# Hybrid decoder trunk, one core: queries and keys of two of four retention heads by Strassen's block form

## The reference

```
xn = rmsnorm(x) * ln_gain
q, k, v, z_a, x_b, z_b, g_a, g_b = split(xn @ w_in)
q, k = rope(q), rope(k) * 256**-0.5             # 4 heads; q, k 256 wide, v 512 wide
A = group_norm(retention(q, k, v, state)) * silu(z_a)   # 128-token chunks, a decaying 256 x 512 state a head
B = rglru(causal_conv4(x_b)) * silu(z_b)                # width 1536
x = x + (sigmoid(g_a) * (A @ w_a) + sigmoid(g_b) * (B @ w_b)) @ w_o
```

## Time and profile before

| | |
|---|---|
| median of 3 runs | 1893.31 us (1891.85 to 1895.51) |
| profiled execution, span from first to last instruction | 1889.0 us (its own time outside the span is not shown) |
| TensorE busy | 1872.9 us, 99% |
| VectorE busy | 1306.7 us, 69% |
| ScalarE busy | 827.0 us, 44% |
| GpSimd busy | 298.6 us, 16% |
| moved by DMA | 264.06 MB, mean 140 GB/s |

### The profile page before, as it was taken

How to read it: one execution, slowest core, us unless ns; L and a number is a source line. 1 busy time by engine, 2 the same in 40 slices (tenths; PEclk the granted TensorE clock), 3 DMA queues, 4 the chain that set the end, 5 groups by cost and what they waited for, 6 DMA issues and landing times.

```text
span 1889.0 us, 32627 instructions
## 1 busy us (share of the span) xinstructions
PE 1872.9 (99%) x13004; PEld 1755.0 (93%) x13004; DVE 1306.7 (69%) x2260; ACT 827.0 (44%) x1352; POOL 298.6 (16%) x417
## 2 busy tenths in 40 slices
PE   9999999999999999999999999999999999999998
PEld 8899898898899999999998988988988999999997
DVE  7775665665766877866797656657557678878575
ACT  5432322423436776543444324234124377766334
POOL 2220120120231210100132201202102422001010
PEclk9999999999999999999999999999999999999999
DMA  6444534553443333543655445534444534337253
GB/s 220 137 129 159 179 132 130 163 180 110 150 147 96 104 99 99 155 134 105 199 175 162 148 124 170 178 110 152 168 119 146 167 97 107 96 93 183 90 167 116
DMA packets 119958, 264.06 MB, mean 140 GB/s; under 512 B 12510, under 2 KB 52942, under 8 KB 119678
## 3 DMA queue, kind: packets, MB, share of 16 engines
q1 hardware_dynamic: 87950, 159.94, 27.3%
q0 software_dynamic: 31712, 102.04, 17.5%
q10 hardware_dynamic: 144, 0.00, 0.0%
HBM read 203.11 MB, written 49.12 MB: 134 GB/s over the span
## 4 chain that ended last, share of the span: by engine, by line
PE 87%; DVE 5%; ACT 3%; DMA 2%; DVEq 1%; issue 1%; ACTq 1%; SPq 0%
PE bank L2414 19%; PE bank L2416 19%; PE bank L2415 19%; PE bank L2508 4%; PE bank L2509 4%; PE bank L2510 4%; PE bank L2778 2%; PE bank L2781 2%; PE bank L2780 2%; DMA w_raw<-in_w_units 2%; PE sums L2526 2%; PE sums L2508 1%; PE sums L2510 1%; PE sums L2509 1%; PE sums L2641 1%
## 5 line engine op out<-in xcount | busy, mean ns | idle before, releaser
L2414 PE MATMUL bank<-xn_hi,w_hi 128*128 128x296 f32 (+1 forms) x2016 | 603.5, 299 | 1.1 <-DVEq L2324 0.5
L2416 PE MATMUL bank<-xn_lo,w_hi 128*128 128x296 f32 (+1 forms) x2016 | 598.9, 297 | 0.0
L2415 PE MATMUL bank<-xn_hi,w_lo 128*128 128x296 f32 (+1 forms) x2016 | 598.1, 297 | 0.0
L2414 PEld LDWEIGHTS bank<-xn_hi,w_hi 128*128 128x128 f32 x2016 | 379.0, 188 | 8.4 <-issue 6.0
L671 ACT ACTIVATE w_hi<-w_raw 128x1024 fp32r<-128x1024 f32 x219 | 230.2, 1055 | 349.0 <-DMA w_raw<-in_w_units 346.4
L2415 PEld LDWEIGHTS bank<-xn_hi,w_lo 128*128 128x128 f32 x2016 | 379.5, 188 | 0.9
L2416 PEld LDWEIGHTS bank<-xn_lo,w_hi 128*128 128x128 f32 x2016 | 378.6, 188 | 0.0
L681 DVE TENSOR_TENSOR w_lo<-w_raw,w_hi 128x1024 fp32r<-128x1024 f32 x219 | 268.4, 1229 | 59.1 <-ACT w_hi L671 52.5
L2414 PE MATMUL bank<-oa_hi,w_hi 128*128 128x296 f32 (+1 forms) x512 | 153.7, 300 | 0.0
L2415 PE MATMUL bank<-oa_hi,w_lo 128*128 128x296 f32 (+1 forms) x512 | 151.9, 297 | 0.0
L2416 PE MATMUL bank<-oa_lo,w_hi 128*128 128x296 f32 (+1 forms) x512 | 151.7, 296 | 0.0
(11 more groups left out here) (347 smaller groups left out, 3846.1 us busy)
## 6 DMA issues: line engine op xcount, KB each, us to landing
w_raw<-in_w_units SPq DMA_DIRECT2D x189, 512.0 KB, 3.7
w_raw<-in_w_units SPq DMA_DIRECT2D x151, 256.0 KB, 3.4
S<-in_state_ret POOLq DMA_DIRECT2D x64, 512.0 KB, 4.8
out_ret_s<-S POOLq DMA_DIRECT2D x64, 512.0 KB, 6.2
w_raw<-in_w_units POOLq DMA_DIRECT2D x20, 256.0 KB, 4.9
vst<-v_scr SPq DMA_DIRECT2D x8, 512.0 KB, 4.1
out_ret_p<-Sp POOLq DMA_DIRECT2D x8, 512.0 KB, 5.9
v_scr<-vtok_hi SPq DMA_DIRECT2D x16, 160.0 KB
```

Source lines behind the costliest of these rows:

```text
L2414: pe.matmul(ps, w_hi[:, slot, cols], x_hi, start=first, stop=False)
L2415: pe.matmul(ps, w_lo[:, slot, cols], x_hi, start=False, stop=False)
L2416: return pe.matmul(ps, w_hi[:, slot, cols], x_lo, start=False, stop=last)
```

## The change

For the third and the fourth head of each layer (`PAIR_HEADS = (2, 3)`), queries and keys are made by the block form: first the pair of key tiles, then the pair of query tiles, 7 x 12 matmuls each in place of 2 x 48. On all 592 tokens in both layers.

- **Token sums.** The four sums are made once a layer on VectorE: two steps at the end of the first head, six among the second head's queries and keys (`token_sum`), in six planes over `vo` and the value places. POOL stores four of them to DRAM in the second head (`store_sums`), and both ScalarE and VectorE wait for these stores before the values' tail is written.
- **Reload.** At the end of the second and third head, after the last transposes, POOL loads the four planes (592 KB each) back into the same places (`load_sums`). ScalarE makes four high parts; VectorE makes the low parts of DIFF and MIX2 after the second unit of W_A and those of EDGE and LAST after the fourth.
- **Weights.** SP loads 14 raw parts in place of four units. POOL adds into S1 of the keys' pair behind `load_sums`, into S3 of the keys' behind the last state stores, into S1 of the queries' ahead of the next head's state loads, and into S3 of the queries' behind them.
- **End of a head before a changed one.** ScalarE and VectorE split A11, S1, S2, A12 of the keys in place of three units, VectorE also makes S2 + S1 and S4 + S2.
- **In the head.** `high_pairs` and `low_pairs` are written out for ScalarE and VectorE. The keys are turned (`turned`) among the queries' parts, the queries after the last product. `keys(0)` waits for the keys alone; the wait for the queries moves to before `cross(0)`.
- `act.sem_inc` and `dve.sem_inc` for units held by pairs become a drain that increments.
- `product`, `part_high`, `part_low`, `part_add`, `right_low`, `both_sums` move up, three snapshot semaphores become one, and the loop in "B" becomes `block_pair`.

The diff, cut to its core:

```diff
-TILE_PAIRS = KT // 2
+PAIR_HEADS = (2, 3)
+TURN_PAIRS = 2 * len(PAIR_HEADS)
+TILE_PAIRS = TURN_PAIRS + KT // 2
...
             if by_pair(u):
-                dve.sem_inc(unit_lo, 1)
+                dve.drain().then_inc(unit_lo, 1)
                 return
...
@@ SP
+                if at % 16 == 0 and at // 16 in PAIR_HEADS and at < HEADS * 16:
+                    load_parts(l, head_pairs(at // 16))
@@ POOL
+                def load_sums(h):
+                    pool.wait_ge(sums_out, (l + 1) * SUMS * 16)
+                    wait_job(pool, "R", l, h, ("oT", 4))
+                    for plane in (DIFF, MIX2, EDGE, LAST):
+                        pool.dma_start(sum_raw[:, plane, :, :].rearrange("p k t -> p (k t)"), sum_scr[plane])\
+                            .then_inc(again_in[plane], 16)
...
+                    if h in PAIR_HEADS:
+                        add_part(head_pairs(h)[1], S1)
                     for n in range(S_RING):
                         load_state(n)
+                    if h in PAIR_HEADS:
+                        add_part(head_pairs(h)[1], S3)
+                    if h + 1 == PAIR_HEADS[0]:
+                        store_sums()
+                        pool.wait_ge(sums_out, (l + 1) * SUMS * 16)
...
                     pool.dma_start(dst, Sp[:, :, :]).then_inc(sp_out, 16)
+                    if h + 1 in PAIR_HEADS:
+                        load_sums(h)
+                        add_part(head_pairs(h + 1)[0], S1)
                     for pair in range(S_RING // PAIRED, DEC_BATCH // PAIRED):
...
                             store_state(n)
+                    if h + 1 in PAIR_HEADS:
+                        add_part(head_pairs(h + 1)[0], S3)
                     for s in range(S_RING):
                         pool.wait_ge(s_out[s], (hh * uses(s) + uses(s)) * 16)
@@ ScalarE, in the head
+                    def high_pairs():
+                        keys, queries = head_pairs(h)
+                        split_hi(act, "R", l, h, 0)
+                        for two in (keys, queries):
+                            keep_sum(two, A11, bank[two % 2], 0, HALF)
+                            keep_sum(two, S1, bank[2], 1, HALF)
+                            part_high(two, S3)
+                            keep_sum(two, S2, bank[two % 2], 2, HALF)
+                            part_high(two, S4)
+                            part_high(two, A22)
+                            if two == keys:
+                                part_high(queries, A11)
+                                part_high(queries, S1)
+                                last_block(keys)
+                                part_high(queries, S2)
+                                part_high(queries, A12)
+                        split_hi(act, "R", l, h, 1)
+                        high_keys(1)
+                        last_block(queries)
+                        split_hi(act, "R", l, h, 2)
+                        high_queries(2)
+                        split_hi(act, "R", l, h, 3)
@@ ScalarE, end of the head before
+                    if h + 1 in PAIR_HEADS:
+                        for plane in (DIFF, MIX2, EDGE, LAST):
+                            act.wait_ge(again_in[plane], l * AGAIN + 16 * (PAIR_HEADS.index(h + 1) + 1))
+                            act.activation(sum_lohi[:, SUMS + plane, :, :], sum_raw[:, plane, :, :], ACT.Copy)\
+                               .then_inc(right_hi, 1)
+                        for part in (A11, S1, S2, A12):
+                            part_high(head_pairs(h + 1)[0], part)
@@ VectorE, in the head
+                    def turned(two, at, between):
+                        one, two_minus = result_of(two, 0), result_of(two, 1)
+                        dve.drain()
+                        dve.tensor_tensor(qk[:, at, :], one, cos, MUL)
+                        dve.tensor_tensor(qk[:, at + 1, :], one, sin, MUL)
+                        dve.wait_ge(c21_ready, l * TILE_PAIRS + two + 1)
+                        dve.tensor_tensor(rot[:, 0, :], two_minus, sin, MUL)
+                        dve.tensor_tensor(rot[:, 1, :], two_minus, cos, MUL)
+                        between()
+                        dve.drain()
+                        dve.tensor_tensor(qk[:, at, :], qk[:, at, :], rot[:, 0, :], ADD)
+                        dve.tensor_tensor(qk[:, at + 1, :], qk[:, at + 1, :], rot[:, 1, :], SUB)
+                        dve.drain()
+                    def low_pairs():
...
+                        for two in (keys, queries):
+                            x = bank[two % 2]
+                            if two == keys:
+                                part_low(two, S3)
+                            part_low(two, S4)
+                            both_sums(two, A12, bank[3], 0, c11_ready, 0, a0, b0)
+                            part_low(two, A22)
+                            both_sums(two, S3, x, 1, c22_ready, 1, a1, b1)
+                            if two == keys:
+                                part_low(queries, A11)
+                            else:
+                                dve.drain().then_inc(freed("R", (("proj", 1), 1)), 2)
+                                split_lo(dve, "R", l, h, 1)
+                            both_sums(two, S4, bank[2], 2, c12_ready, 0, a1, b1)
+                            if two == keys:
+                                part_add(queries, S2, S1)
+                                part_low(queries, S1)
+                                part_add(queries, S4, S2)
+                                part_low(queries, S2)
+                                part_low(queries, A12)
+                                turned(keys, 2, lambda: part_low(queries, S3))
+                                dve.drain().then_inc(qk_ready, 1)
+                        dve.drain().then_inc(freed("R", (("proj", 1), 0)), 2)
+                        turned(queries, 0, lambda: split_lo(dve, "R", l, h, 2))
+                        with_decay()
+                        dve.drain().then_inc(qk_ready, 1)
+                        dve.wait_ge(ret_stored, hh + 1)
+                        split_lo(dve, "R", l, h, 3)
@@ VectorE, after each unit of W_A
                         split_lo(dve, "R", l, h, 12 + two)
+                        if h + 2 == PAIR_HEADS[0] and two >= 2:
+                            token_sum(two - 2)
+                        if h + 1 in PAIR_HEADS:
+                            keys = head_pairs(h + 1)[0]
+                            if two == 1:
+                                sum_low(h + 1, DIFF)
+                                sum_low(h + 1, MIX2)
+                            elif two == 2:
+                                part_low(keys, A11)
+                                part_add(keys, S2, S1)
+                                part_low(keys, S1)
+                            elif two == 3:
+                                sum_low(h + 1, EDGE)
+                                sum_low(h + 1, LAST)
+                                part_add(keys, S4, S2)
+                                part_low(keys, S2)
+                                part_low(keys, A12)
@@ TensorE
+                def block_pair(two, columns, right, lows, jobs, nth):
...
+                    product(two, A11, x, xn_hi[:, 0:4, a0:b0], xn_lo[:, 0:4, a0:b0], True)
...
+                    product(two, S1, y, diff_h, diff_l, True)
+                    pe.wait_ge(snap_ready, pairs * 3 + 1)
+                    wait_right(2)
+                    product(two, S2, x, mix2_h, mix2_l, False)
...
+                    product(two, A12, z, xn_hi[:, 4:KT, a0:b0], xn_lo[:, 4:KT, a0:b0], True)
+                    pe.wait_ge(snap_ready, pairs * 3 + 3)
+                    wait_right(3)
+                    product(two, S3, x, edge_h, edge_l, False)
+                    product(two, S4, y, xn_hi[:, 4:KT, a1:b1], xn_lo[:, 4:KT, a1:b1], False)
+                    pe.wait_ge(c22_ready, pairs + 1)
+                    wait_right(4)
+                    product(two, A22, x, last_h, last_l, False)
...
                     values(0)
-                    pe.wait_ge(qk_ready, hh * 2 + 2)
+                    pe.wait_ge(qk_ready, hh * 2 + (1 if h in PAIR_HEADS else 2))
                     keys(0)
...
                     project("R", l, h, ("proj", 8), 8)
+                    pe.wait_ge(qk_ready, hh * 2 + 2)
                     cross(0)
```

More of the change, by code:

```diff
@@ L288, in by_pair, with head_pairs @@
     l, at = divmod(u, UNITS_LAYER)
+    if at < HEADS * 16:
+        return at // 16 in PAIR_HEADS and at % 16 < 4
     return O_AT <= at < O_AT + 2 * (OUT_PAIRS[l] - STORED_PAIRS)
+def head_pairs(h):
+    keys = 2 * PAIR_HEADS.index(h)
+    return keys, keys + 1
 def taken_count(l, which):
@@ L304, in ring_places @@
         for at in range(UNITS_LAYER):
-            for first, pairs in ((B_AT, range(TILE_PAIRS)), (O_AT, range(TILE_PAIRS, LAYER_PAIRS[l]))):
+            for first, pairs in (*((16 * h, head_pairs(h)) for h in PAIR_HEADS), (B_AT, range(TURN_PAIRS, TILE_PAIRS)),
```

(29 more changed lines are left out.)

388 lines of the change are left out of this document (221 added, 167 removed).

## The result

The changed kernel takes 1910.21 us (median of 4 runs, 1906.96 to 1910.96), the kernel before 1892.82 us beside it (1891.85 to 1895.51): a ratio of 1.0088, 95% interval 1.0074 to 1.0102. It is slower by 17 us, outside my range of 1886 to 1901. The profiled execution spans 1908.8 us against 1889.0. In all runs made later an execution's own time is 1.7 to 2.2 us above its span, so the execution profiled before took about 1891 us, some 2 us less than its median: that is why the spans differ by 19.8 us and the medians by 17.4. The prediction's step of 4.3 us from span to median mixed two executions, which does not touch the sum.

The account below looks back on a forecast made before the run. TensorE, busy for 99% of the span, was taken to bound the kernel. A gain of 12.4 us less four heads' waits of 1.56 + 0.65 + 0.74 us gave -0.6 us: 1892.7 us, whole range 1886 to 1901.

Parts of the forecast that it names:

- step of 4.3 us from span to median: Whole kernel: the median of runs, 1893.3 us, lies 4.3 us above the profiled span, a distance kept for the forecast.
- What bounds the kernel; the gain: TensorE bounds the kernel, busy 99% of the span; fewer matmuls in the four changed heads save 12.4 us.
- Token sums, reload: Sums in the first and second head cost nothing; reloading their planes is hidden, with some 4 us in hand.
- First wait, 1.56 us: At the keys' S2, VectorE's low part comes too late for TensorE: 1.56 us lost in each changed head.
- Second wait: At the queries' S2: raw S4 lands in 4.7 us, the addition starts at 14.5, S2 is just in time.
- parts stand behind the state loads: Rival at the queries: raw S4 lands after 6.4 us, 4.6 us lost a head, 1899.1 us; slower had chance 0.28.
- The alternation of the queues: DMA engines alternate queues by packet, so raw parts on SP's queue land near the quiet time; the S2 wait goes.
- S3 0.65, S4 0.74 us: At the queries' S3 and S4 in each changed head, VectorE's low parts come 0.65 and 0.74 us late.
- slower: Whole kernel slower by over 0.2%, chance 0.28; priced at 1899.1 us.

Follow-up runs that it names:

- the first experiment: State loads of the changed heads issued behind both queries' adding loads (S1 and S3) instead of between them, against the changed kernel: 1906.72 us.

## Why the prediction was wrong

**What bounds the kernel; the gain.** Right. With the waits taken away the stretches come to within 0.3 to 0.6 us of 22.84, and the four together are 10.5 us shorter than before, of the 12.4 forecast.

**Token sums, reload.** Right at zero. ScalarE had made the first two high parts by 261.0 and all four by 264.5; VectorE asked for the first two at 264.8, so 3.8 us were in hand where I counted 4. No stage outside of the two named moved by more than 0.6 us.

**First wait, 1.56 us.** Right in mechanism: VectorE ran the chain as written, and 1.78, 1.78, 1.73 and 1.74 us were measured. It was a little too small, and not additive: a later start gives the loads time.

**Second wait: this is the step that failed.** I took 4.7 us for the landing of the queries' raw S4, between 3.1 and 6.4; it was 7.7. The addition began 17.9 us after the head's start, not 14.5, though VectorE was ready for it at 13.7, and the queries' S2 lost 2.97, 3.90, 3.55 and 1.98 us where I had 0. My rival "parts stand behind the state loads" had the mechanism and the sign; I gave its price the size of the worst row before, 6.4 us, as its ceiling. With the state loads out of the stretch the same load takes 2.6 to 3.6 us, so they are what made it late. Why it was 7.7 and not 6.4 is argued and not tested: the row of 6.4 us is of a kernel that moves 4.76 MB in a window of 26.3 us, and the changed one moves 7.1 MB in 29.8, with nine parts of 256 KB for each pair where there were two units of 512 KB. More stands on the queues together with the states, and a landing taken from the emptier queue is no upper bound for the fuller one.

The alternation of the queues that I weighed fits the rows, and would have given the sign had I gone on to bytes. From 287.9 to 295.6 the two queues moved 552 and 419 packets, nearly in turn, but 2.03 and 0.76 MB: 3.7 KB a packet for the states, 1.8 KB for the parts. SP's queue got 0.76 MB / 7.7 us, 99 GB/s, and nearly three parts in a row take those 7.7 us. The Trainium skill (page DMA: Bandwidth & Descriptors, section Queues, rings and completion order) has each DMA engine take the queues in turn, one packet at a time. The counts of packets agree with that roughly, 552 to 419; no run here changed the packets' sizes. That a landing is then near the quiet one was my own step, and it is wrong: 7.7 us.

**A term that was missing: the clock.** After the wait at the queries' S2 the granted clock fell in all four heads and cost 1.5 us each time, 6.1 us in all. Nothing in my working priced a wait at more than its length. For the third head of layer 0 the account closes so: 22.84 + 1.78 + 2.97 + 1.53 + 0.31 (at S4) = 29.43, measured 29.75. The four heads together: 7.0 for the first wait, 12.4 for the second, 6.1 for the clock, 1.2 at S4 and 1.7 in small gaps are 28.4 us, against a gain of 12.4: the 16.0 us lost.

**S3 0.65, S4 0.74 us.** Mostly hidden in the changed kernel, since TensorE was late and slow: nothing at S3, 0.28 to 0.62 at S4 in three heads. With the state loads moved alone, S3 is in time and S4 0.5 to 0.6 late; with the first wait gone too, 0.55 and 0.61. So the link was right, but it is VectorE's order of work and needs no late landing: with prompt landings I had counted on the first wait alone. Both are gone with VectorE's other order.

**The gates' stage, 4.0 us.** I had nothing here. Its code is the same in all of these kernels. Over the nine others with block heads it took 46.15 to 48.00 us in layer 0 and 45.47 to 48.01 in layer 1, with no relation to what was changed that I can see; in the run where only the state loads moved it was 46.15 and 45.47, below the kernel before (46.41, 45.84). It hangs on adding loads that land just in time, and I read the 4.0 us as their scatter from one execution to the next. That is argued from these rows, not tested by an experiment of its own; the cause of the 4.0 us stays open. The medians, 17.4 us apart, leave only 1.4 for it beside the 16.0 of the heads.

**Chances.** I gave 0.28 to slower and priced it at 1899.1. With a landing of 7.7 us the rival's own formula gives a start 17.5 us after the head's start and 5.9 us a head, and with the clock's 1.5 some 7.5: 1911. That it meets the measured time is partly chance, since the waits at S3 and S4 were hidden and the gates' 4 us are not in it.

## What to carry to other kernels

When a change shortens the life of each buffer, list every burst that another queue drops into that stretch; a landing time read from the old kernel is no upper bound for the new one. Put bursts that nobody waits for where the weights have slack; moving one within the tight stretch mostly picked another victim here. A wait of TensorE of 2 us or more can cost more than its length: here 16 of 21 cost 1.4 to 1.9 us more, for the clock.

## What the runs showed of the hardware

The clock was the surprise. In these traces the block heads and gates' stages hold 21 waits of TensorE of 1.98 to 5.35 us. With 16 of them the granted clock fell, and 8 to 16 of the matmuls behind the wait ran at the lower level. The loss was 1.4 to 1.6 us in 15 of them, whatever the wait's length (1.5 after 1.98 us and after 3.92), and 1.9 after the one of 5.35. With the other 5 (2.03, 2.50, 2.84, 3.10 and 3.13 us) nothing fell, and none of the waits of 1.1 to 1.84 us was followed by a fall of its own. What decides between them these rows do not show. In 12 of the 16 the fall came when TensorE was at work again, up to 1.4 us after; in the other 4 it came while TensorE still stood. The wait of 5.35 us, in the run with one head, ends at 432.13:

```profile
429.50:432.00 2.50, 0.00 (x0) 0.00 (x0) 1.40 (x3) 0.00 (x0) 0.16 (x1) 0.50 1.03 239
```

TensorE is busy for none of these 2.5 us, and the granted clock is 0.50 already. For the wait of 3.66 us at the values' start, in the first experiment, the fall comes after it:

```profile
308.00:312.00 4.00, 3.78 (x12) 2.79 (x13) 3.81 (x7) 1.35 (x2) 0.00 (x0) 0.70 0.34 92
```

TensorE is busy for 3.78 of 4 us there, at a granted clock of 0.70: a stretch that looks busy can still be lost time.

Two waits removed one at a time gave 3.5 and 2.8 us, both together 13.4: as long as one burst or one late link was left, the next in line took over the wait.
